# A chunked scan with eight steps: the read products, the state product and the late modulation move within a step

## The reference, cut to what matters

```python
mod_x = silu(c) @ ada_w[l] + ada_b[l]            # 1024 -> 6144, split in six
...
def step(s, inp):                                # rwkv_scan, one token
    r_t, k_t, v_t, kk_t, a_t, w_t = inp
    sa = einsum("dbhij,dbhj->dbhi", s, kk_t)
    s = s * w_t[..., None, :] - sa[..., :, None] * (kk_t * a_t)[..., None, :] \
        + v_t[..., :, None] * k_t[..., None, :]
    y = einsum("dbhij,dbhj->dbhi", s, r_t) if readout else None
    return s, y
...
y = fft2(uf, axes=(1, 3), norm="ortho").real     # fourier_mix, then an rms norm
```

## Time and profile before

| | us |
|---|---|
| median of the timed runs | 1356.27 |
| the profiled execution's own time | 1358.7 |
| its span | 1356.7 |
| of this: before the first step of the scan's loop | 178.3 |
| the eight iterations of the scan's loop | 218.1 |
| from the scan's end to the end | 960.3 |
| TensorE busy | 1251.9 |
| VectorE busy | 539.8 |
| ScalarE busy | 360.0 |
| GpSimd busy | 124.6 |

### The profile page before, as it was taken

One profiled execution on the slowest core, in us unless ns is written; L12 is line 12 of the kernel. 1 busy time (PEld: TensorE's weight loads), 2 busy tenths in 40 slices (PEclk: granted clock), 3 DMA queues, 4 the chain that ended last, 5 costly groups with the idle time before them and its releaser, 6 DMA issues.

```text
span 1356.7 us, 23863 instructions
## 1 busy us (share of the span) xinstructions
PE 1251.9 (92%) x10420; PEld 901.9 (66%) x10420; DVE 539.8 (40%) x1103; ACT 360.0 (27%) x850; POOL 124.6 (9%) x139
## 2 busy tenths in 40 slices
PE   6999887888979899999989999999999769999996
PEld 2445776777768788888868887656687654455433
DVE  1258133335442799990030722674162240111113
ACT  2435243345420322111011212455430112101101
POOL 0004244333200000110000000000000100000000
PEclk9999999899999999999989999999999969999999
DMA  9700013232254343434333333111122367999992
GB/s 395 291 0 32 7 50 106 72 104 73 73 200 173 124 178 133 161 135 169 128 131 145 124 124 125 63 63 62 63 97 92 146 288 290 430 427 428 425 429 80
DMA packets 21095, 225.06 MB, mean 166 GB/s; under 512 B 2624, under 2 KB 5824, under 8 KB 6528
## 3 DMA queue, kind: packets, MB, share of 16 engines
q1 hardware_dynamic: 20592, 222.17, 41.7%
q0 software_dynamic: 256, 1.06, 0.2%
q10 hardware_dynamic: 144, 0.31, 0.1%
HBM read 220.38 MB, written 1.05 MB: 163 GB/s over the span
## 4 chain that ended last, share of the span: by engine, by line
PE 86%; DVE 4%; DMA 3%; ACT 3%; issue 2%; POOL 1%; SPq 0%; ACTq 0%; DVEq 0%
PE ps L665 37%; PE ps L1264 7%; PE ps L1074 6%; PE ps L786 5%; PE ps L1133 5%; PE ps L1308 4%; PE ps L788 2%; PE ps L1179 2%; DMA mem<-experts 2%; PE ps L1275 2%; PE ps L1245 2%; PE ps L1150 2%; PE ps L764 1%; PE ps L643 1%; PE ps L895 1%
## 5 line engine op out<-in xcount | busy, mean ns | idle before, releaser
L665 PE MATMUL ps<-mem 128*128 128x256 f32 (+2 forms) x2096 | 522.3, 407 | 12.2 <-DVE mem L2036 4.2
L665 PEld LDWEIGHTS ps<-mem 128*128 128x128 f32 x2096 | 399.7, 192 | 123.8 <-issue 50.3
L2017 DVE SCALAR_TENSOR_TENSOR mem<-ps,mem 128x189 f32<-128x189 f32 (+2 forms) x352 | 148.2, 431 | 14.8 <-ACT mem L1604 3.9
L786 PE MATMUL ps<-mem 64*64 64x64 f32 (+1 forms) x2176 | 111.0, 245 | 24.1 <-DVE mem L1822 8.5
L788 PE MATMUL ps<-mem 64*64 64x64 f32 (+1 forms) x2176 | 112.1, 246 | 7.9 <-issue 7.9
L786 PEld LDWEIGHTS ps<-mem 64*64 64x64 f32 x2176 | 91.3, 142 | 39.7 <-issue 19.0
L1264 PE MATMUL ps<-mem 128*64 128x512 f32 x512 | 111.6, 592 | 1.2 <-DMA mem<-experts 0.7
L788 PEld LDWEIGHTS ps<-mem 64*64 64x64 f32 x2176 | 92.0, 142 | 8.6 <-issue 8.6
L1369 ACT ACTIVATE mem<-ps 128x512 f32<-128x512 f32 (+4 forms) x111 | 71.3, 658 | 96.4 <-PE ps L788 72.6
L1264 PEld LDWEIGHTS ps<-mem 128*64 128x64 f32 x512 | 37.3, 137 | 73.7 <-issue 73.0
L2242 DVE TENSOR_TENSOR mem<-ps,mem 128x512 f32<-128x512 f32 x8 | 5.5, 693 | 188.3 <-PE ps L1264 188.3
(11 more groups left out here) (266 smaller groups left out, 1332.9 us busy)
## 6 DMA issues: line engine op xcount, KB each, us to landing
mem<-experts SPq DMA_DIRECT2D x48, 2048.0 KB, 17.3
mem<-weights SPq DMA_DIRECT2D x44, 2048.0 KB, 8.1
mem<-late_ada SPq DMA_DIRECT2D x16, 1024.0 KB, 5.3
mem<-weights SPq DMA_DIRECT2D x3, 1536.0 KB, 6.6
mem<-tokens SPq DMA_DIRECT2D x1, 2048.0 KB, 12.3
mem<-mem SPq DMA_DIRECT2D x32, 64.0 KB, 5.0
mem<-consts SPq DMA_DIRECT2D x1, 1519.0 KB, 23.6
out<-mem SPq DMA_DIRECT2D x1, 1024.0 KB, 4.8
```

Source lines behind the costliest of these rows:

```text
L665: last = mm(bank(j % banks)[:, 0:nn], w[:, kc, c * P:(c + 1) * P], rr(kc), start=kc == 0, stop=kc == KD - 1)
L786: mm(out[hp, 0, j], lhs[hp, 0, j], rhs[hp, 0, j], start=True, stop=True)
L2017: n(stt(out=o, in0=src[:, r0 + dy:r1 + dy, c0 + dx:c1 + dx], scalar=prm("ffn_conv", tap * 2 * NG + j), in1=o, op0=ALU.mult, op1=ALU.add))
```

## The change

Three things move, in all engines' programs at once. (1) In TensorE's program `squares_of_far(i)` comes straight after `spread_solution(i-1, 1)`, then `read_out` or `late_piece`, and only then `turned(i)`; `fourths_of_far` writes banks 0 and 1 instead of 2 and 3. (2) `state(i-1)` goes from the end of iteration i to the head of iteration i + 1. (3) The late modulation is cut by rows instead of by columns: a half is 512 rows by 512 columns, again 1 MB, in 8 MATMULs of 512 columns; two halves add up in bank 7, one ScalarE copy of 512 columns takes them out, and `turn_late` turns all four blocks at once. Half 0 stands between `squares_of_near` and `second_factor`, half 1 after `squares_of_far` (chunks 0 to 3) or after `turned` (4 to 7). VectorE masks `AT` before `A`, keeps `M2T` ahead of the staging of the next reads, and keeps the grams behind it.

```diff
-        JOBS = {"prep_made": (("removalsT", "removals", "A2", "A2T", "A4", "Q1", "W8", "M", "MT", "turned", "M2", "M2T",
+        JOBS = {"prep_made": (("removalsT", "removals", "A2", "A2T", "A4", "Q1", "W8", "M", "MT", "M2", "M2T", "turned",
                                "M4T"),
...
-                    sp.wait_ge(S("mod_turned"), W_IN + 2 * STEPS)
+                    sp.wait_ge(S("mod_turned"), W_IN + STEPS)
...
+            def late_piece(i, half):
+
+                pe.wait_ge(S("late_ada_in"), 16 * (2 * i + half + 1))
+                if half == 0:
+                    pe.wait_ge(S("mod_kept"), i + 1)
                     if i == 0:
-                        waits(0, "M4T_kept")
-                for kc in range(KD):
-                    lane = kc % 4
-                    last = mm(bank(7)[32 * lane:32 * lane + 32, 0:PIECE], cond_act[:, kc, :], late_ada[:, kc, :],
-                              start=kc < 4, stop=kc >= 4)
+                        waits(0, "reads_kept", "gram_kept")
+                for lane in range(KD // 2):
+                    last = mm(bank(7)[32 * lane:32 * lane + 32, :], cond_act[:, 4 * half + lane, :], late_ada[:, lane, :],
+                              start=half == 0, stop=half == 1)
                 last.then_inc(S("mod_rows"), 1)
...
+                else:
+                    waits(s - 1, "M4T_kept")
                 if s < READ_FROM:
                     product("removalsT", prep_bank(s, 0), keys, reads[:, :, :, BOTH], 2 * C)
...
                 if s >= 2:
-                    waits(s - 1, "M4T_kept")
+                    waits(s - 1, "gram_kept", "reads_kept")
                 product("removals", prep_bank(s, 1), reads[:, :, :, FIRST], keys)
...
+            def squares_of_far(s):
+                waits(s, "M_kept", "MT_kept")
+                if s < READ_FROM:
+                    waits(s, "X0_kept")
+                product("M2", prep_bank(s, 0), B1, B2)
+                product("M2T", prep_bank(s, 1), B2, B1)
+
             def turned(s):
                 if s >= READ_FROM:
-                    waits(s, "M_kept")
+                    waits(s, "M2_kept")
                     product("X0", prep_bank(s, 0), W8, WR[:, :, :, C:3 * C], 2 * C)
-                waits(s, "MT_kept")
+                waits(s, "M2T_kept")
...
             def fourths_of_far(s):
                 waits(s, "M2_kept", "M2T_kept")
-                product("M4T", prep_bank(s, 1), B3, B4)
+                if s >= READ_FROM:
+                    waits(s, "X0_kept")
+                product("M4T", prep_bank(s, 0), B3, B4)
...
             for i in range(1, STEPS + 1):
+                if i >= 2:
+                    state(i - 2)
                 if i < STEPS:
                     removals(i)
                 if i >= 2:
-                    turn_piece(i - 2, 1)
+                    turn_late(i - 2)
...
                     squares_of_near(i)
+                late_piece(i - 1, 0)
                 second_factor(i - 1)
                 if i <= NJ:
                     token_spectrum(i - 1, 0)
-                else:
-                    late_piece(i - 1, 0)
...
-                if i <= NJ:
-                    late_piece(i - 1, 0)
-                elif i < STEPS:
+                if NJ < i < STEPS:
                     inverse_of_near(i)
...
                 spread_solution(i - 1, 1)
-                turn_piece(i - 1, 0)
                 if i < STEPS:
-                    turned(i)
-                    state(i - 1)
                     squares_of_far(i)
                 if i - 1 >= READ_FROM:
                     read_out(i - 1)
-                late_piece(i - 1, 1)
+                else:
+                    late_piece(i - 1, 1)
+                if i < STEPS:
+                    turned(i)
+                if i - 1 >= READ_FROM:
+                    late_piece(i - 1, 1)
                 if i < STEPS:
                     fourths_of_far(i)
-            turn_piece(STEPS - 1, 1)
+            turn_late(STEPS - 1)
...
             def keep_removals(s):
+                dve.wait_ge(*turn("removalsT_copied", s))
+                masked(B2, AO, near).then_inc(turns_of("AT_kept"), 1)
                 dve.wait_ge(*turn("removals", s))
...
             for i in range(STEPS):
+                if i >= 2:
+                    keep_state(i - 2)
                 keep_removals(i)
...
+                keep(i, "M2T", B4)
                 if 1 <= i < STEPS - 1:
                     stage_reads(i + 1)
-                keep_grams(i)
-                if i >= 1:
-                    keep_state(i - 1)
-                keep(i, "M2T", B4)
-                keep_raised(i, "M4T", 1, M4TI)
                 if READ_FROM <= i + 1 < STEPS:
                     stage_own_reads(i + 1)
+                keep_grams(i)
+                keep_raised(i, "M4T", 0, M4TI)
```

More of the change, by code:

```diff
@@ L281, in two_blocks @@
         gate_w = m1.take(RW)
-        late_ada = m1.take(KD, PIECE)
+        late_ada = m1.take(KD // 2, 2 * PIECE)
         at_h = Places(mem, arena, total)
@@ L325, in two_blocks @@
         KF = Places(mem, after_h, arena + KD * TB).take(2, 2, NJ, 2 * C)
-        late_rows = wd.rearrange("p (a c) -> p a c", a=2)
+        late_rows = wd
         both_roots = Places(mem, m1_root, m1_root + 2 * TB)
@@ L746, in token_spectrum @@
                     pe.wait_ge(S("spectrum_kept"), 4)
+                    if j == 0:
+                        waits(0, "reads_kept", "gram_kept")
                     if j >= 1:
@@ L753, in token_spectrum, with turn_late @@
                     last.then_inc(S("mixed"), 1)
-            def late_piece(i, piece):
-                pe.wait_ge(S("late_ada_in"), 16 * (2 * i + piece + 1))
-                if piece == 0:
+            def late_piece(i, half):
+                pe.wait_ge(S("late_ada_in"), 16 * (2 * i + half + 1))
+                if half == 0:
                     pe.wait_ge(S("mod_kept"), i + 1)
                     if i == 0:
-                        waits(0, "M4T_kept")
-                for kc in range(KD):
-                    lane = kc % 4
-                    last = mm(bank(7)[32 * lane:32 * lane + 32, 0:PIECE], cond_act[:, kc, :], late_ada[:, kc, :],
-                              start=kc < 4, stop=kc >= 4)
-                last.then_inc(S("mod_rows"), 1)
[L768 to L773, removed]
+                        waits(0, "reads_kept", "gram_kept")
+                for lane in range(KD // 2):
+                    last = mm(bank(7)[32 * lane:32 * lane + 32, :], cond_act[:, 4 * half + lane, :], late_ada[:, lane, :],
+                              start=half == 0, stop=half == 1)
+                last.then_inc(S("mod_rows"), 1)
+            def turn_late(i):
+                pe.wait_ge(S("mod_rows_kept"), W_IN + i + 1)
+                for c in range(4):
+                    last = mm(bank(7)[:, 2 * c:2 * c + 2], late_rows[:, c * P:(c + 1) * P], cst("pick"),
                               start=True, stop=True)
@@ L953, in _ @@
             channel_spectrum(1)
-            turned(0)
             squares_of_far(0)
@@ L957, in _ @@
             channel_spectrum(3)
+            turned(0)
             fourths_of_far(0)
             for i in range(1, STEPS + 1):
+                if i >= 2:
+                    state(i - 2)
                 if i < STEPS:
@@ L1437, in keep_mod @@
             def keep_mod(i):
-                act.wait_ge(S("mod_turned"), 2 * i + (W_IN + 2))
-                A(mod[:, 4 * i + 16:4 * i + 20, :], bank(7)[:, 256:264].rearrange("p (n o) -> p n o", o=2), ACT.Copy)\
+                act.wait_ge(S("mod_turned"), i + (W_IN + 1))
+                A(mod[:, 4 * i + 16:4 * i + 20, :], bank(7)[:, 0:8].rearrange("p (n o) -> p n o", o=2), ACT.Copy)\
                     .then_inc(S("mod_kept"), 1)
@@ L1451, in key_factors, with keep_late @@
                           bias=ka_rest[:, j:j + 1]).then_inc(S("key_factors"), 1)
[L1453 to L1456, removed]
+            def keep_late(i):
+                act.wait_ge(S("mod_rows"), 2 * i + (W_IN + 2))
+                act.wait_ge(S("mod_turned"), W_IN + i)
+                A(late_rows, bank(7), ACT.Copy).then_inc(S("mod_rows_kept"), 1)
             def keep_lora(n):
@@ L1533, in _ @@
             keep_spectrum(3)
+            keep_turned(0)
             def keep_mixed(j):
@@ L1552, in _ @@
                     keep_part_of_near(i)
-                if i <= NJ:
-                    keep_piece(i - 1, 0)
-                elif i < STEPS:
+                if NJ < i < STEPS:
                     keep_inverse(i)
@@ L1578, in _ @@
                     keep_read(i - 1)
-                keep_piece(i - 1, 1)
+                else:
+                    keep_late(i - 1)
+                if i < STEPS:
+                    keep_turned(i)
+                if i - 1 >= READ_FROM:
+                    keep_late(i - 1)
             keep_mod(STEPS - 1)
@@ L1854, in keep_removals @@
                 masked(B1, over_banks(prep_bank(s, 1), C), near[:, ::-1]).then_inc(turns_of("A_kept"), 1)
```

(7 more changed lines are left out.)

24 lines of the change are left out of this document (7 added, 17 removed).

## The result

Six timed runs of each kernel gave 1347.45 us for the changed one and 1356.62 us for the one before; the ratio is 0.994 with a 95% interval of 0.9924 to 0.9956. So the change is worth 7 to 9 us. Forecast were 16, at 1340, with 1330 to 1355 as the range: the direction and the range hold, the size is about half. One run of the kernel before, taken beside a_again, b_late_x2 and a_all_thin, lasted 3258.6 us, in the slow state, and is in none of the ratios.

The account below looks back on a forecast made before the run. TensorE bounds the kernel, its instruction blocks held behind queued data. Transfers' -15.6 us and the small terms' -0.2 sum to -15.8: the span goes from 1356.7 to 1340.9, the median to 1340.5, stated as 1340; range 1330 to 1355.

Parts of the forecast that it names:

- The price of those stalls: Scan loop before: 13.3 us of TensorE idle in "issue" waits plus 10.3 us lost to lowered clock, together 23.6 us.
- (a): Moved transfers in the scan loop: 8 of 23.6 us of stalls and half clock stay, so 15.6 us less.
- (g): Last iteration: X2 and X3 wait for the late transfer too, the last turn is longer; 0.8 us more.
- the two edges: Iterations 3 and 4: block asked for within 0.2 us of the first packet; stall 0 or 1.4, 0 or 2.1 us.
- (b): Late modulation: fewer, wider MATMULs and turning all 8 at once; 2.0 us less.
- (c): TensorE's waits for VectorE's masks: AT ahead of A 3.0 us less, longer turn in iteration 6 1.7 less.
- (d): `removals` waits for M4T, kept behind the grams, at four heads, 0.65 us each; 2.6 us more.
- (e): X3 waits for VectorE's copy of X2 without the late piece as cover, 0.7 us x 3; 2.1 us more.
- (f): `read_out` waits behind `spread1` for VectorE, 0.2 x 3, and `spread0` for X3's copy, 0.1 x 4; 1.0 us more.
- Only moved, or weren't the cause: Rival: loop stalls stay as large, only the small terms change; 1356 us, chance 0.14.
- Both transfers starve TensorE: Rival: head stalls stay, half 1's transfer adds one before each `spread0`; 23 us more, 1379 us, chance 0.08.
- The other two: Rivals: all loop stalls freed, 1332.5 us, chance 0.18; half 0 late in the last three chunks, 1342, within the forecast's 0.60.

Follow-up runs that it names:

- a_again: The changed kernel again, unchanged, beside the kernel before on another chip; 1349.3 us, 0.9948 of before.
- b_late_x2: The kernel before with only the first late piece of each step moved ahead of `second_factor`; 1362.95 us, 1.0051 of before.
- a_all_thin: a_all with each `late_ada` transfer cut from 1 MB to 64 KB, result wrong; 1328.1 us, 0.9795 of before.
- b_thin: The kernel before with each `late_ada` transfer cut from 1 MB to 64 KB, result wrong; 1337.1 us, 0.9868 of before.
- b_again: The kernel before, unchanged, for a second profile; 1356.8 us, 1.0006 of before.
- a_pad32: The changed kernel with 64 already satisfied waits (32 instructions) put in TensorE's program ahead of the first removals; 1347.1 us, 0.9946 of before.
- a_thin: The changed kernel with each `late_ada` transfer cut to a sixteenth, result wrong; 1334.4 us, 0.9849 of before.
- b_at: The kernel before with only VectorE's masking of AT moved ahead of A; 1359.3 us, 1.0017 of before.
- a_all: The changed kernel with half 0 at the first piece's old places, M4T kept ahead of the grams, half 1 ahead of `read_out` and `turned`; 1333.4 us, 0.9852 of before.

## Why the prediction was half right

**What bounds the kernel, and the cause of the stalls: right.** The trace of before was read as instruction blocks behind data. b_thin (19.7 us below b_again, 17.9 by its ratio), b_again (the same five MATMULs) and a_pad32 (the waits move by the 32 instructions put in) show it.

**"The price of those stalls", 23.6 us: too high.** This is the first term that was mis-sized. Taking the transfers away brought 17.9 us by the ratio (13 to 23), of which 1.8 at most are the wait for the late piece, which the 23.6 do not hold. Two things were wrong in it. The sum took one execution's stalls for every run's: the loop of that execution was 22.1 us longer than b_thin's, that of b_again 17.7. And it took all "issue" time and all half clock of five iterations for the transfers'. b_thin keeps 1.5 us of "issue" and, at a clock of 0.97, some 5 us of half clock, most of it around the wait for VectorE's masks in iteration 6, whose half clock the prediction had put into the stalls' price.

**(a), what stays: 8 us forecast, 12.4 by the ratios (7 to 17), 12.6 and 11.7 by the loops.** This is the second. The profile shows 6.9 of "issue" (forecast 5.5), 3.4 of half clock (2.5; a_thin keeps 1.7 of such) and 1.4 of waiting for the late piece, which stands under (g); the rest has no label. The iterations were right but one: forecast were iteration 1 0.5 (measured 0.77 in W8), 2 0.8 (0.93 in spread0), 3 0 or 1.4 (0.66 in spread0), 4 0 or 2.1 (2.10 in keysT), 5 0.7 (none), 7 1.8 (1.23 in A2T), and the small ones at the head. But I gave the two edges even odds, since I had the edge at the first packet. By a_pad32 it is nearer the issue, so both boundaries lie well inside. In after the second had the half clock behind it, (1 - 0.89) x 30.5 = 3.4 us; in a_again it had none, and as much stood elsewhere.

With both terms the sum is -17.9 + 12.4 = -5.5 in place of -15.6: 10 us of gain that did not come, of which the small terms below give back 2.5, so that 7 to 8 are missing. The two loops of each kernel give -22.1 + 12.6 = -9.5 and -17.7 + 11.7 = -6.0. The failed step is this difference of two prices; its direction holds in both pairs, its size is known to some 5 us.

**What stays open.** Counted by labels, the stalls did what was forecast: "issue" fell by 6.9 us and half clock, as (1 - clock) x length, by about 10, together more than 15.6. But the loop fell by 12.2, since other waits grew (X3 4.0, M4T 3.0, `read_out` 1.9) by more than the masks' fell (5.0), and TensorE's busy time fell by less than its half clock. A stall that goes uncovers a wait that it had hidden, as b_at shows the other way round. So how much of the shortfall belongs to the stalls and how much to the small terms depends on which is taken away first, and only the total is firm.

**The small terms: -0.2 us forecast; with thin transfers the loop is 2.7 us shorter, and half clock makes that much.** (b) 2.0 less: only the turning came, 1.4 us (8 times 2 x 0.61 less 1.05); 8 MATMULs of 512 columns took 1.06 us, not the 0.96 taken from the 16 at the start:

```profile
182.29 1.06 PE L765 MATMUL ps<-mem 128*32 128x512 f32 x8
...
202.68 1.05 PE L773 MATMUL ps<-mem 128*128 128x2 f32 x8
```

(c) the masks' waits went from 8.5 to 3.5 us, forecast 3.8, so right as a wait; b_at shows that its worth hangs on what stands behind it. The norm's wait in iteration 6 is 1.78, forecast 1.94. (d) 0.65 x 4 = 2.6: measured 3.0 (0.64 to 1.00 each), right. (e) 0.7 x 3: 0.88 x 3, and 1.35 in the last iteration, which I had under (g). (f) 0.2 x 3: 0.46 x 3, since `read_out` waits for ScalarE's 1.02 us copy, which I hadn't looked at, and not for VectorE; the 0.1 x 4 of `spread0` did not come. (g) 0.8 more: the last iteration took 22.4 for 22.5 us although `state(6)` is in it; its clock was 1.00 for 0.92.

Of the signs named, the clock of 0.97 or more held except in iteration 4, and the iterations 1 to 3 took 21.8, 24.2 and 24.6 us, where some 23 was forecast.

**The rivals.** "Only moved, or weren't the cause" is out on the cause, but a good part of the stalls did move. "Both transfers starve TensorE" had a mechanism that did occur, at about a third of its price: behind half 1's transfer stood 4.5 us of waits and 3.4 of half clock, not 23, and its edge is the very one that decided in iterations 3 and 4. The other two did not happen.

**The notes.** The Trainium skill's sentence that the crossing is "mostly hidden" ("Runtime: NRT & Kernel Launch", "Instruction fetch mechanics") does not hold here: 1.3% of the kernel before hung on it. On the turns between queues ("DMA: Bandwidth & Descriptors", "Queues, rings and completion order") the prediction said that the rows speak against them; that was more than they show. 143 records of data pass ahead of one block asked for near their start, which is 9 for each of the 16 engines, and the page lets a turn hold some 9 to 17 descriptors. Whether a record of the trace is a packet or a descriptor of the page no run here tells.

## What to carry to other kernels

Where a tensor program is unrolled and dense, read every "issue" wait in the middle of a product against the DMA queues: a large transfer is better released where the engine spends its time on few instructions than just ahead of a dense stretch; what the transfers cost fell from 17.9 us (before) over 12.4 (after) to 5.3 (a_all), though other waits changed with it. Price stalls of this kind by a run without the transfer and by several runs, not by the labels of one profile, and expect little from removing a wait that stands ahead of such a stall. The largest gain in this series, a_all's 14 us over after, came from plain waits of one engine for another, which the stalls had drawn the eye away from. And when a cover is moved (here the late piece from behind X2), the next product's copy is what is late.

## What was not expected of the hardware

- A block asked for, by the count of instructions, some 0.25 us after the start of a 1 MB transfer's issue, and 0.7 us before its first packet, still came behind all of it (block at 238.5 us, issue at 233.95, in a_pad32).
- Two profiles of one kernel differ by 4.4 us in a loop of 216, with the long "issue" waits at the same MATMULs; about half of it is idle time and half the clock.
- The length of a wait does not tell what the clock does behind it. 1.2 and 1.6 us in iteration 7 of after and of a_again left it at 1.00, and so did 2.4 us in iteration 4 of a_again and 2.6 us in iteration 2 of b_again; 2.1 us in iteration 4 of after and 1.5 us in iteration 3 of a_again were followed by 0.50.
